# Low parts of the input weights ahead of the modulation sums, values ahead of the keys, and a key latent spread inside the last input tile

## The reference, cut to what matters

```python
x = layer_norm(x, ln_emb_g, ln_emb_b)
z = x @ w_in[i]
xs, gs, cq, ckv, kr, gm = jnp.split(z, IN_SPLIT_POINTS, axis=-1)   # 512, 512, 256, 128, 64, 512
ys = s5_branch(xs, ..., w_glu[i], b_glu[i]) * jax.nn.silu(gs)      # a complex scan over positions
ym = mla_branch(cq, ckv, kr, cos, sin, q_norm_g[i], w_uq[i], kv_norm_g[i], w_ukv[i]) * jax.nn.silu(gm)

# in mla_branch
q = (rms_norm(cq, q_norm_g) @ w_uq).reshape(bsz, seqlen, MLA_HEADS, QK_DIM)    # 128 plain + 64 rotary
kv = (rms_norm(ckv, kv_norm_g) @ w_ukv).reshape(bsz, seqlen, MLA_HEADS, QK_NOPE + V_HEAD)
k_nope, v = kv[..., :QK_NOPE], kv[..., QK_NOPE:]
k_rope = rotary(kr, cos, sin)

# in second_block, the modulation
ada = jax.nn.silu(c) @ w_ada[i] + b_ada[i]
```

## Time and profile before

| | |
|---|---|
| median of 3 runs | 2211.8 us (2209.73 to 2216.22) |
| the profiled execution as a whole | 2214.04 us |
| its span | 2211.3 us |
| granted TensorE clock, mean | 0.986 of full speed |
| busy share of TensorE, VectorE, ScalarE, GpSimd | 96%, 56%, 35%, 56% |

### The profile page before, as it was taken

One profiled execution on the slowest core, in us unless ns is written; L12 is line 12 of the kernel. 1 busy time (PEld: TensorE's weight loads), 2 busy tenths in 40 slices (PEclk: granted clock), 3 DMA queues, 4 the chain that ended last, 5 costly groups with the idle time before them and its releaser, 6 DMA issues.

```text
span 2211.3 us, 28169 instructions
## 1 busy us (share of the span) xinstructions
PE 2119.7 (96%) x11208; PEld 1653.5 (75%) x11208; DVE 1230.6 (56%) x1476; ACT 777.4 (35%) x1188; POOL 1239.1 (56%) x826
## 2 busy tenths in 40 slices
PE   8989989999998999999999999998899999999998
PEld 3878835878875885578767788786788888888886
DVE  6999836541768115510168226867766666652424
ACT  6222342340117005620174442145454554431211
POOL 1485812047873663337656754473788888844441
PEclk9999989999998999999999999999999999999999
DMA  7462460042332321001221225323122222154112
GB/s 290 141 145 94 110 214 29 1 164 95 104 100 76 120 77 46 28 29 67 55 47 58 96 108 206 122 76 126 43 82 86 86 86 86 58 191 143 48 39 76
DMA packets 66033, 212.68 MB, mean 96 GB/s; under 512 B 15159, under 2 KB 17511, under 8 KB 64719
## 3 DMA queue, kind: packets, MB, share of 16 engines
q1 hardware_dynamic: 52624, 152.73, 20.7%
q10 hardware_dynamic: 9040, 36.45, 4.5%
q0 software_dynamic: 4240, 21.70, 3.5%
HBM read 162.73 MB, written 46.17 MB: 94 GB/s over the span
## 4 chain that ended last, share of the span: by engine, by line
PE 85%; DVE 6%; ACT 3%; POOL 2%; issue 2%; DMA 1%; SPq 0%; ACTq 0%; DVEq 0%
PE ps L3304 22%; PE ps L2916 17%; PE ps L3423 11%; PE ps L2938 6%; PE ps L3228 4%; PE ps L3337 3%; PE ps L2881 3%; PE ps L3375 2%; PE ps L355 2%; PE ps L525 1%; PE ps L513 1%; PE ps L378 1%; PE ps L1036 1%; PE ps L507 1%; PE ps L538 1%
## 5 line engine op out<-in xcount | busy, mean ns | idle before, releaser
L1589 POOL TENSOR_TENSOR w_parts<-front,sb_zero 128x1024 fp32r<-128x1024 f32 x69 | 140.7, 2039 | 282.1 <-PE ps L3423 117.7
L1664 POOL TENSOR_TENSOR up_parts<-front,up_parts 128x512 fp32r<-128x512 f32 x120 | 194.5, 1628 | 70.4 <-ACT up_parts L1966 70.3
L3423 PE MATMUL ps<-ffn_parts,w_parts 128*128 128x512 f32 x1008 | 230.3, 389 | 1.5 <-DVE front L2842 1.5
L1594 POOL TENSOR_TENSOR w_parts<-front,w_parts 128x1024 fp32r<-128x1024 f32 x75 | 208.5, 2780 | 22.2 <-ACT w_parts L2121 7.5
L3423 PEld LDWEIGHTS ps<-ffn_parts,w_parts 128*128 128x128 f32 x1008 | 189.0, 188 | 41.7 <-issue 2.6
L3304 PE MATMUL ps<-t_high,up_parts 128*128 128x512 f32 x640 | 205.6, 392 | 5.8 <-ACT back L1973 4.6
L2916 PE MATMUL ps<-h_high,w_parts 128*128 128x512 f32 x672 | 187.6, 394 | 0.6 <-PE ps L3228 0.6
L1474 POOL TENSOR_TENSOR front<-front,sb_csilu 128x1024 f32<-128x1024 f32 x48 | 102.2, 2129 | 114.4 <-DMA front<-w_ada 114.4
L3304 PE MATMUL ps<-h_high,up_parts 128*128 128x512 f32 x480 | 154.6, 389 | 1.5 <-DVE back L2610 1.5
L3304 PEld LDWEIGHTS ps<-t_high,up_parts 128*128 128x128 f32 x640 | 121.4, 190 | 31.9 <-issue 6.5
L2916 PEld LDWEIGHTS ps<-h_high,w_parts 128*128 128x128 f32 x672 | 124.0, 188 | 25.8 <-issue 1.4
(11 more groups left out here) (429 smaller groups left out, 4870.8 us busy)
## 6 DMA issues: line engine op xcount, KB each, us to landing
front<-w_ada SPq DMA_DIRECT2D x48, 512.0 KB, 3.7
front<-w_up SPq DMA_DIRECT2D x44, 512.0 KB, 4.4
front<-w_down SPq DMA_DIRECT2D x22, 512.0 KB, 3.5
front<-w_in SPq DMA_DIRECT2D x16, 512.0 KB, 4.8
front<-w_out SPq DMA_DIRECT2D x16, 512.0 KB, 4.9
residual<-back ACTq DMA_DIRECT2D x2, 4096.0 KB, 15.6
front<-w_gates SPq DMA_DIRECT2D x16, 512.0 KB, 4.1
gates<-back SPq DMA_DIRECT2D x16, 512.0 KB, 3.6
```

Source lines behind the costliest of these rows:

```text
L1589: pool.tensor_tensor(high, raw, zero[:, 0:1].to_broadcast((P, PAGE)), ALU.add)\
L1594: pool.tensor_tensor(low, raw, high.bitcast(F32), ALU.subtract).then_inc(S("w_split"), 1)
L1664: pool.tensor_tensor(parts[:, BANK:], src, parts[:, 0:BANK].bitcast(F32), ALU.subtract)\
L3423: mm = pe.matmul(ps[:, 2 * m + nt, :], parts[n % 2 + w_][:, at:at + P], half_of(AR[kk % 4 + x_], nt), start=k == 0 and q == 0, stop=k == N ...
```

## The change

`in_low` of a tile now stands ahead of the modulation sum in GpSimd's loop, and the column that closes a sum moves to k = 6 of the tile's second pass (in tile 15 the two columns stand at k = 4 and 7). The key latent's spread moves into tile 15, between its second and third pass; the query latent's moves from behind the fourth state group to behind the third. The eight value products now come ahead of the four key tiles, and the keys use the pairs 5, 0, 2, 5. ScalarE's two gains for the query latent move in among its copies of the values. Rotary queries exchange their banks, and the gated product uses banks 4 to 7; the attention waits for its last sigmoid at its second item. On GpSimd's queue the scan's output goes to DRAM ahead of the copies of the rotary key, and the gate tiles are read back last. No instruction that computes is added or removed.

```diff
--- before.py
+++ after.py
@@ -1150,6 +1150,7 @@
         TEMPS_2 = (cols(48 * PAGE + 512, 49 * PAGE + 512), page(32), page(32))
         LATENT_ROOT = {"kv_norm": cols(49 * PAGE + 512, 49 * PAGE + 768), "q_norm": cols(33 * PAGE, 33 * PAGE + 256)}
         STATE_BANK = (0, 1, 2, 3)
+        K_BANK = (5, 0, 2, 5)
         TEMPS_3 = (page(12), page(13), page(14))
 
         BLOCKS_WIN = 32
@@ -1499,7 +1500,6 @@
                     .then_inc(S("u_landed"), 16)
 
             for i in range(6, N_IN):
-                ada_sum(i - 4)
                 if i in (8, 9):
                     gather(4 * i - 30)
                     gather(4 * i - 29)
@@ -1507,6 +1507,7 @@
                     pool.wait_ge(S("z_tile"), 8)
                     pool.memset(TM, 0.0).then_inc(S("pool_step"), 1)
                 in_low(i)
+                ada_sum(i - 4)
                 if i == 7:
                     pool.wait_ge(S("x_in_dram"), 16)
                     pool.wait_ge(S("dve_step"), DVE_STEP["cp_table"])
@@ -1524,11 +1525,10 @@
             ada_sum(13)
             ada_sum(14)
             ada_sum(15)
-            pool.wait_ge(S("gate_out0"), 64)
-            pool.wait_ge(S("gate_out1"), 64)
-            pool.wait_ge(S("z_tile"), N_IN)
-            pool.dma_start(GS, silu_dram[0:4].rearrange("k p t -> p k t")).then_inc(S("silu_back"), 16)
-            pool.dma_start(GM, silu_dram[4:8].rearrange("k p t -> p k t")).then_inc(S("silu_back"), 16)
+            pool.wait_ge(S("ssm_ps_read"), 32)
+            for s in range(STEP):
+                pool.dma_start(y_dram.rearrange("(g c) t -> c g t", c=GC)[:, :, s * CHUNKS:(s + 1) * CHUNKS],
+                               UU[s * GC:(s + 1) * GC, :, :]).then_inc(S("y_in_dram"), 16)
             pool.wait_ge(S("z_free"), N_IN)
             pool.wait_ge(S("dve_step"), DVE_STEP["cm_zero"])
             for half in range(2):
@@ -1536,12 +1536,13 @@
                 pool.dma_start(page(47)[64 * half:64 * half + 64, :], KR[64:128, :]).then_inc(S("kr_landed"), 16)
             pool.dma_start(CM[:, SEQ - P:SEQ], t["causal"]).then_inc(S("cm_landed"), 16)
 
-            pool.wait_ge(S("ssm_ps_read"), 32)
-            for s in range(STEP):
-                pool.dma_start(y_dram.rearrange("(g c) t -> c g t", c=GC)[:, :, s * CHUNKS:(s + 1) * CHUNKS],
-                               UU[s * GC:(s + 1) * GC, :, :]).then_inc(S("y_in_dram"), 16)
             pool.wait_ge(S("y_in_dram"), 16 * STEP)
             pool.dma_start(YF, y_dram.rearrange("(k p) t -> p k t", p=P)).then_inc(S("yf_landed"), 16)
+            pool.wait_ge(S("gate_out0"), 64)
+            pool.wait_ge(S("gate_out1"), 64)
+            pool.wait_ge(S("z_tile"), N_IN)
+            pool.dma_start(GS, silu_dram[0:4].rearrange("k p t -> p k t")).then_inc(S("silu_back"), 16)
+            pool.dma_start(GM, silu_dram[4:8].rearrange("k p t -> p k t")).then_inc(S("silu_back"), 16)
 
             pool.memset(zero[:], 0.0).then_inc(S("pool_step"), 1)
             pool.wait_ge(S("pool_step"), POOL_STEP["zero"])
@@ -1811,16 +1812,15 @@
                     act.wait_ge(S("dve_step"), DVE_STEP["angle_reduced"])
                     act.activation(SIN, COS, ACT.Sin).then_inc(S("act_step"), 1)
                     act.activation(page(47), COS, ACT.Sin, scale=0.5).then_inc(S("act_step"), 1)
-            latent_gain_act(act, 1)
-            latent_gain_act(act, 2)
-
+            for kt in range(8):
+                act.wait_ge(*T("kv_tile", kt + 1))
+                act.activation(VT[:, kt, :], ps[:, kt % 4, :], ACT.Copy).then_inc(S("kv_free"), 1)
+                if kt in (3, 5):
+                    latent_gain_act(act, kt // 2)
             for m in range(4):
-                act.wait_ge(*T("kv_tile", m + 1))
-                act.activation(KNH[m], two(2 * (m % 2)), ACT.Copy).then_inc(S("kv_free"), 1)
+                act.wait_ge(*T("kv_tile", 8 + m + 1))
+                act.activation(KNH[m], two(K_BANK[m]), ACT.Copy).then_inc(S("kv_free"), 1)
             ada_read(0, 16)
-            for kt in range(8):
-                act.wait_ge(*T("kv_tile", 4 + kt + 1))
-                act.activation(VT[:, kt, :], ps[:, kt % 4, :], ACT.Copy).then_inc(S("kv_free"), 1)
             act.wait_ge(S("y_in_dram"), 16 * STEP)
             for m in range(4):
                 act.wait_ge(*T("q_tile", m + 1))
@@ -1833,7 +1833,7 @@
                 act.wait_ge(*T("glu_tile", m + 1))
                 if m >= 2:
                     act.wait_ge(S("glu_used"), m - 1)
-                act.activation(page(20 + m % 2), two(2 * (m % 2)), ACT.Sigmoid, bias=V("b_glu", m))\
+                act.activation(page(20 + m % 2), two(4 + 2 * (m % 2)), ACT.Sigmoid, bias=V("b_glu", m))\
                     .then_inc(S("glu_sig"), 1)
             act.activation(na_sum[:, 0:1], eps[:, 0:1], ACT.Exp)
             attention_act(act, "mla", BUFS_1, mla_items()[0], MLA_SCALE)
@@ -2424,8 +2424,8 @@
 
             dve.wait_ge(S("z_tile"), 16)
             for m in range(4):
-                dve.wait_ge(*T("kv_free", m + 1))
-                dve.tensor_tensor(KNL[m], two(2 * (m % 2)), KNH[m].bitcast(F32), ALU.subtract).then_inc(S("k_low"), 1)
+                dve.wait_ge(*T("kv_free", 8 + m + 1))
+                dve.tensor_tensor(KNL[m], two(K_BANK[m]), KNH[m].bitcast(F32), ALU.subtract).then_inc(S("k_low"), 1)
 
             dve.wait_ge(S("kr_landed"), 64)
             dve.wait_ge(S("ssm_ps"), 32)
@@ -2439,8 +2439,8 @@
                 dve.tensor_tensor(QNL[m], two(2 * (m % 2)), QNH[m].bitcast(F32), ALU.subtract).then_inc(S("q_low"), 1)
             for m in range(2):
                 dve.wait_ge(*T("qr_tile", m + 1))
-                tt(page(47), two(4 * m), COS, ALU.mult)
-                tt(page(22), two(4 * m + 2), SIN, ALU.mult)
+                tt(page(47), two(4 - 4 * m), COS, ALU.mult)
+                tt(page(22), two(6 - 4 * m), SIN, ALU.mult)
                 dve.sem_inc(S("qr_free"), 1)
                 tt(page(47), page(47), page(22), ALU.add)
                 for i in range(2):
@@ -2962,7 +2962,9 @@
                 in_products(bank, (IN_LOW[i],), XH, start=True).then_inc(S("win_low_used"), 1)
                 if i == IN_FIRST:
                     pe.wait_ge(S("z_free"), 3)
-                in_products(bank, (IN_HIGH[i],), XH, between={4: {0: 0, 4: 1}, 5: {}, 15: {0: 11, 7: 12}}.get(i, {0: i - 4}))
+                in_products(bank, (IN_HIGH[i],), XH, between={4: {0: 0, 4: 1}, 5: {}, 15: {4: 11, 7: 12}}.get(i, {6: i - 4}))
+                if i == N_IN - 1:
+                    latent_spread_pe(pe, "kv_norm")
                 in_products(bank, (IN_HIGH[i],), XL, stop=True).then_inc(S("z_tile"), 1)
 
             pe.wait_ge(S("ones_set"), 1)
@@ -3016,7 +3018,6 @@
             latent_sums_pe(pe, 1)
             pe.wait_ge(S("dve_step"), DVE_STEP["states_ready"])
             pe.wait_ge(S("tm_landed"), 16 * (STEP - 1))
-            latent_spread_pe(pe, "kv_norm")
             for r in range(4):
                 if r < 2:
                     pe.wait_ge(S("z_free"), 15 + r)
@@ -3042,37 +3043,40 @@
                 if r == 0:
                     latent_sums_pe(pe, 2)
                     ada_column(13, "ada_used")
-                elif r == 3:
+                elif r == 2:
                     latent_spread_pe(pe, "q_norm")
 
             pe.wait_ge(S("norm_ready"), tiles_to("kv_norm", 1))
             b = B_UKV
             block_landed(B_UKV)
+            for kt in range(8):
+                if kt in (0, 2):
+                    pe.wait_ge(S("ssm_ps_read"), 30 + kt)
+                if kt >= 4:
+                    pe.wait_ge(*T("kv_free", kt - 3))
+                pe.matmul(ps[:, kt % 4, :], CKV[:, kt * P:(kt + 1) * P], ring[:, b % RING, BANK:2 * BANK],
+                          start=True, stop=True).then_inc(S("kv_tile"), 1)
+                if kt in (3, 7):
+                    ada_column(14 + kt // 4, "ada_used")
+            for m in range(4):
+                if m == 0:
+                    pe.wait_ge(S("norm_scaled"), tiles_to("q_norm", 2))
+                elif m < 3:
+                    pe.wait_ge(*T("kv_free", 4 + 2 * m))
+                else:
+                    pe.wait_ge(*T("kv_free", 9))
+                    pe.wait_ge(*T("k_low", 1))
+                tile(K_BANK[m], b % RING, lambda k: CKV, kts=1, at=m * P).then_inc(S("kv_tile"), 1)
+            pe.wait_ge(*T("kv_tile", 12))
+            pe.sem_inc(S("w_used"), 1)
+
+            pe.wait_ge(S("norm_ready"), tiles_to("q_norm", 2))
+            block_landed(B_UQ)
             for m in range(4):
                 if m < 2:
-                    pe.wait_ge(S("ssm_ps_read"), 30 + 2 * m)
-                if m >= 2:
-                    pe.wait_ge(*T("kv_free", m - 1))
-                    pe.wait_ge(*T("k_low", m - 1))
-                tile(2 * (m % 2), b % RING, lambda k: CKV, kts=1, at=m * P).then_inc(S("kv_tile"), 1)
-                if m in (0, 2):
-                    ada_column(14 + m // 2, "ada_used")
-            for kt in range(8):
```

(37 more changed lines are left out.)

2 lines of the change are left out of this document (1 added, 1 removed).

## The result

| | before | after |
|---|---|---|
| median of the comparison's runs | 2213.63 us (2209.73 to 2217.57) | 2218.77 us (2211.81 to 2223.55) |
| ratio, 95% interval | | 1.0020 (1.0011 to 1.0029) |
| the profiled execution, its span | 2214.04, 2211.3 us | 2211.81, 2208.9 us |
| start of the attention in it | 367.90 | 369.71 |

The account below looks back on a forecast made before the run. TensorE, 96% busy, was taken as the bound, so only its idle time and low-clock work could be won. Attention at 356.2 instead of 367.90 gave 11.7 us: span 2199.6, execution 2202.3, median 2200.1, range 2193.5 to 2206.5.

Parts of the forecast that it names:

- Tile 6: Input product: its 5.21 us wait for the weights' low part goes, with 1.5 us of clock, 6.7 us together.
- the column's new wait of about 1 us: Tile 6's second product, k = 6: TensorE waits about 1 us for the modulation sum, bounds 0 and 2.5.
- What this is worth is decided on VectorE: Key latent's spread in tile 15: TensorE waits about 4 us for VectorE's reciprocal, which ends at 254.3.
- Part 1's gain of 0.6 us: Low parts before modulation sums: states start at 261.7 against 262.31, leaving 0.6 us; bounds 2.3 and −0.7.
- Query latent, values, keys: Behind the states: query spread waits for nothing; these stages end at 279.8, 287.0 and 293.9, without waits among the keys.
- rival (d): Values and keys: ScalarE's gains delay the values by over 2 us, clock falls; gain about 7 us, chance 0.04.
- A new wait of 4.3 us: First query subtraction: TensorE waits from 300.8 to 305.1 behind the rotary key's turning, plus 1.7 us of clock.
- rival (a): First query subtraction: rotary copies land at 303.8, wait 10.1 us, gain only 5.9 us, time 2205.9; chance 0.12.
- Behind the attention nothing changes: From the attention on: TensorE is the bound, so all 11.7 us gained ahead should arrive at the end.
- (b): Key latent's spread: VectorE is no gate, being through by 250; gain 17.8 us, time 2194.0, chance 0.08.
- (c): Columns at k = 6: late sums stop TensorE in all ten tiles, 2.5 us each; time 2220.7, chance 0.04.
- sum of 11.7 us: Total gain up to the attention, which starts at 356.2 instead of 367.90.

Follow-up runs that it names:

- part2_only: after with GpSimd's loop, the columns and both spreads put back as in before; values first, new banks and new DMA order stay: ratio 1.0018 to before.
- second_mended: after with GpSimd's loop, columns and spreads as before; output in halves, rotary copies between, rotary key turned behind query subtractions: ratio 0.9933 to before.
- scan_first: after with ScalarE's high-part copy for tile 10 moved behind the eight evacuations of the scan's input: ratio 1.0006 to before.
- after_again: after once more without an edit, for a second profile: ratio 1.0019 to before.
- turn_later: after with VectorE's five rotary key operations and their wait moved behind the four query subtractions: ratio 0.9985 to before.
- output_in_halves: after with ScalarE's tile 10 copy behind the evacuations, rotary key turned behind query subtractions, output in two halves, rotary copies between: ratio 0.9903 to before.

## Why the prediction was wrong, point by point

- **Tile 6, and the column's new wait of about 1 us:** right (0 and 1.55 us).
- **"What this is worth is decided on VectorE": wrong, the first step that failed.** VectorE was through with the reciprocal at 246.0, not 254.3. I had one profile of before and took its order of events for fixed, within 2 us. In the fourteen profiles of experiments the reciprocal starts between 243.0 and 249.7, and in part2_only and second_mended, where GpSimd's loop is that of before, at 248.5 and 248.0 and not at 252.5. So the 8 us can't be put down to the new order of GpSimd's work alone; what part that has stays open. What I had drawn from the Trainium skill (SBUF — State Buffer, Who interferes with whom) was about the sum of the delays, and I let it fix the gate.
- **Part 1's gain of 0.6 us, states at 261.7:** the number was right (261.47), by luck: the gate that should have made it had no case. Of the 6.7 us won at tile 6, 1.6 went at the column, and 0.5 for the gathers and 3.4 for ScalarE (3.78 against 0.33) in the scan's input, over 90 us ahead of the spread. I had asked for the column and the gathers whether they have room and answered with the mean of GpSimd's waits; I had not asked who waits for the load behind the column. It was ScalarE, with the evacuations queued behind it, and before it had only 0.33 us of wait to show there, which hid that its copy ran at 160.07, 1.4 us ahead of TensorE's arrival. Against part2_only and second_mended, which wait 2.6 and 3.0 us there, the states of after start 5 us earlier; but in the eight profiles with part 1 as it stands and without scan_first they start anywhere from 261.5 to 269.1, so what part 1 is worth stays open.
- **Query latent, values, keys:** right: 279.8, 287.0 and 293.9 forecast, 279.52, 286.86 and 293.97 measured (286.86 and 7.11). Three bank pairs do hide the key chain; rival (d) has no case. But the bound of 1.5 us on the query latent did not hold everywhere: 2.58 us in after_again and 2.01 in turn_later.
- **`w_uq` at no cost: wrong,** 1.79 us (7.5 in part2_only). I gave the load no line of its own, and it took 15.5 us beside the output where before it had taken 8.3.
- **"A new wait of 4.3 us", bounds 2.4 and 6.2: the step that made the forecast wrong.** It was 14.83, and with the same 1.8 us of clock the attention is 13.5 us later than forecast: 1.8 for `w_uq`, 10.5 for this wait, 1.2 in lengths of matmuls taken at 0.43 us. The mechanism was the one named in rival (a), with the copies at 310.6 where (a) had them at 303.8: the wait is three times the 4.3 us of the sum and half as long again as the 10.1 of (a). Two faults lie in the term. First, I took the 19.1 us of twelve transfers at 287 for the time they would need at 281. But moved forward they ran first at 49 and 115 GB/s (280 to 288), and from 283 on beside four weight loads of 0.5 MB; the output was issued 8.9 us earlier than in before (281.00, 289.95) and had landed only 1.6 us earlier (304.76, 306.40), and the last copy, queued behind it, 29.5 us after the first issue. Second, I priced one chain only. ScalarE's wait for the output (L1824) is among the diff's unchanged lines, and so I did not follow it. turn_later shows its price: 5.1 us with the copies off the chain.
- **Behind the attention nothing changes:** right in fourteen profiles; the 4.2 us that the one of after is shorter there stay unexplained.
- **Rivals.** Rival (a) was the right place at the wrong price. (b) was right on VectorE and wrong on the gain, as another gate stood ahead of it. (c), the only one that ended slower, named a mechanism with no case, and the slower result came from elsewhere.

The sum of 11.7 us itself was there to be had, and more: output_in_halves has 19 to 21 us. My 4.3 us of wait and 1.7 of clock are absent in it, and the states are 2.9 us earlier than I forecast.

## What to carry to other kernels

When a stall is removed, list every instruction that TensorE will meet earlier by that much, with the absolute time at which its inputs were ready before; a wait of 0.3 us in the old profile can hide an input that was only just in time. Take a second profile of the old kernel as well: here the wait at that place was 0.3, 2.6 and 3.0 us in three profiles of the same early program. A wait for a semaphore that several chains feed goes only when the last of them is mended, so single edits can each look worthless (here 0.27 to 0.34% over after) and together 1.2%. For transfers, scale by the bytes that all queues will carry in the stretch and by their rate in such pieces, with a wide bound (115 and 194 GB/s here for the same pieces), not by the time that the same transfers took beside other neighbours; and where an output is late, send off what is ready instead of waiting for its last part.

## What the runs showed of the hardware that I had not expected

The scan's output, 2 MB in 512-byte runs from 16 partitions a transfer, kept the DMA engines 88% busy at 115 GB/s (284 to 288 in after), and 84% busy at 194 GB/s as a half alone (272 to 276 in output_in_halves), where a 2 MB load and two of 0.5 MB reached 414 GB/s; a weight load of 0.5 MB beside it took 15.5 us, against 8.3 in before and 4.8 in output_in_halves. Four copies of 256 KB took 16.9 us (median) behind the output on GpSimd's queue and 6.5 us ahead of it. And the same kernel's early stages moved by several microseconds between executions (states at 261.47 and 265.21, attention at 369.71 and 380.44), so one profile's arrival times carry an error of that size, which a forecast of gates has to take in.
